# A norm's first unit multiplied by x times scale: token factor and bias applied behind PSUM

## The reference

```python
def rmsnorm(x, w):
    r = lax.rsqrt(jnp.mean(x32 * x32, axis=-1, keepdims=True) + EPS)
    return (x32 * r).astype(x.dtype) * w

def modulate(h, shift, scale):
    return h * (1 + scale) + shift

def swiglu(h, w_i, w_o):
    g, u = jnp.split(h @ w_i, 2, axis=-1)
    return (jax.nn.silu(g) * u) @ w_o
...
    xl = xl + 0.5 * g1l * swiglu(modulate(rmsnorm(xl, norm_w[0]), sh1l, sc1l), w_ffn1_in, w_ffn1_out)
```

## Time and profile before

| | us |
|---|---|
| median of 3 runs | 2497.06 |
| lowest, highest | 2493.27, 2498.05 |
| profiled execution | 2492.84 |
| its span | 2491.0 |

### The profile page before, as it was taken

How to read it: one execution, slowest core, us unless ns; L and a number is a source line. 1 busy time by engine, 2 the same in 40 slices (tenths; PEclk the granted TensorE clock), 3 DMA queues, 4 the chain that set the end, 5 groups by cost and what they waited for, 6 DMA issues and landing times.

```text
span 2491.0 us, 31535 instructions
## 1 busy us (share of the span) xinstructions
PE 2345.1 (94%) x12784; PEld 1886.1 (76%) x12784; DVE 1146.9 (46%) x1970; ACT 829.7 (33%) x1305; POOL 171.3 (7%) x114
## 2 busy tenths in 40 slices
PE   5999999999999999999999999999997996889998
PEld 3777777775777777777777787689996885658888
DVE  2233222437643222233332224775544767457984
ACT  3222222324342222223222224354444454332233
POOL 1000001014000000000000010310011003000001
PEclk7999999999999999999999998999998997789999
DMA  6444444220124444434444422324552221013433
GB/s 262 172 177 178 176 176 191 84 98 17 52 106 178 181 176 170 177 146 152 179 178 176 159 104 100 119 85 170 187 194 90 90 103 49 1 39 144 154 139 136
DMA packets 48310, 340.13 MB, mean 137 GB/s; under 512 B 5168, under 2 KB 7216, under 8 KB 7344
## 3 DMA queue, kind: packets, MB, share of 16 engines
q1 hardware_dynamic: 47136, 337.15, 36.2%
q10 hardware_dynamic: 1040, 1.05, 0.1%
HBM read 337.13 MB, written 1.05 MB: 136 GB/s over the span
## 4 chain that ended last, share of the span: by engine, by line
PE 88%; DVE 6%; ACT 2%; issue 1%; DMA 1%; POOL 1%; SPq 0%; ACTq 0%; DVEq 0%; POOLq 0%
PE bank L451 44%; PE bank L459 22%; PE bank L852 6%; PE bank L425 4%; PE bank L480 3%; PE bank L693 1%; DMA raw<-stream 1%; PE bank L672 1%; PE bank L503 1%; PE bank L652 1%; DVE h L1619 1%; PE bank L681 1%; PE bank L649 1%; ACT w_hi L900 1%; PE bank L509 1%
## 5 line engine op out<-in xcount | busy, mean ns | idle before, releaser
L1273 DVE TENSOR_TENSOR w_lo<-raw,w_hi 128x1024 fp32r<-128x1024 f32 (+1 forms) x389 | 469.1, 1206 | 1082.6 <-ACT w_hi L900 1082.0
L900 ACT ACTIVATE w_hi<-raw 128x1024 fp32r<-128x1024 f32 (+1 forms) x389 | 403.4, 1037 | 1176.2 <-PE bank L451 1155.8
L451 PE MATMUL bank<-h_hi,w_hi 128*128 128x512 f32 (+1 forms) x2024 | 704.2, 360 | 2.7 <-DVE h_lo L1495 1.4
L451 PE MATMUL bank<-h_lo,w_hi 128*128 128x512 f32 (+1 forms) x2024 | 695.3, 356 | 0.0
L451 PEld LDWEIGHTS bank<-h_hi,w_hi 128*128 128x128 f32 x2024 | 383.6, 190 | 82.8 <-issue 28.0
L459 PE MATMUL bank<-h_hi,w_lo 128*128 128x512 f32 (+1 forms) x2024 | 430.3, 355 | 5.1 <-DVE w_lo L1273 5.1
L451 PEld LDWEIGHTS bank<-h_lo,w_hi 128*128 128x128 f32 x2024 | 383.9, 190 | 52.7 <-issue 0.5
L459 PEld LDWEIGHTS bank<-h_hi,w_lo 128*128 128x128 f32 x2024 | 341.7, 190 | 58.9 <-DVE w_lo L1273 6.0
L451 PE MATMUL bank<-hidden_hi,w_hi 128*128 128x512 f32 (+1 forms) x880 | 296.4, 351 | 2.5 <-ACT w_hi L900 2.5
L451 PE MATMUL bank<-hidden_lo,w_hi 128*128 128x512 f32 (+1 forms) x880 | 293.4, 348 | 0.0
L451 PEld LDWEIGHTS bank<-hidden_hi,w_hi 128*128 128x128 f32 x880 | 167.2, 190 | 33.5 <-issue 13.2
(11 more groups left out here) (217 smaller groups left out, 1945.4 us busy)
## 6 DMA issues: line engine op xcount, KB each, us to landing
raw<-stream SPq DMA_DIRECT2D x317, 1024.0 KB, 4.8
x<-x_in SPq DMA_DIRECT2D x1, 2048.0 KB, 9.9
consts<-consts_in SPq DMA_DIRECT2D x1, 1136.5 KB, 5.5
x<-ctx_in ACTq DMA_DIRECT2D x1, 1024.0 KB, 6.7
out<-x SPq DMA_DIRECT2D x2, 512.0 KB, 3.0
params<-params_in SPq DMA_DIRECT2D x1, 413.5 KB, 3.0
```

The costliest lines, as they stand in the source:

```text
L451: last = nc.tensor.matmul(acc, w_hi[:, buffer, kc, :], v(first_chunk + kc), start=start and kc == n == 0, stop=False)
L900: nc.scalar.activation(w_hi[:, buffer, 0:chunks, :], raw[at % RING][:, 0:chunks, sub * P:(sub + 1) * P], ACT.Copy)\
L1273: nc.vector.tensor_tensor(w_lo[:, buffer, 0:chunks, :], raw[at % RING][:, 0:chunks, sub * P:(sub + 1) * P], w_hi[:, buffer, 0:chunks, :].b ...
```

## The change

For the five norms, the unit behind the norm is no longer multiplied with the normed operand. Since the token factor r is one number per column, (W·(x·r·s + shift)) = r·(W·(x·s)) + W·shift.

- While `x` is still being updated, ACT rounds `x·scale` to a raw high part (`raw_high`, two instructions a chunk where there are 512 columns) and DVE makes its rest (`raw_low`, two also). They go to an area that is free at the time (`RAW_AREA`).
- `delayed_unit` on PE: the first unit, half by half. Behind each chunk's two w_hi matmuls, and before each w_lo matmul, there is one more of 4 columns with the same weights (`shift_parts`: shift split in two parts, for latent and context), which gives the bias. Between the w_hi and the w_lo part of the first half stands the sum of squares (all eight squares are now added on POOL, so one set of one-column matmuls); behind the first half the spread, as 4 matmuls of 128 columns.
- `delayed_norm` on ACT and DVE: the normed operand is still made, for the second unit on. The factor is first copied from PSUM to SBUF (`norm_scale`, which is the tile `rms`). DVE multiplies the even chunks with it, POOL the odd ones (`scale_odd`), in three buffers (`scaled`). In this loop, behind chunk step 4, stand the second unit's second half (ACT converts it at step 3) and what takes the first unit out of PSUM (`then`, `after_bias`): move the bias, multiply with the factor, add the bias; in a SwiGLU `Silu` on ACT stands between.
- `joint_product` now multiplies the second unit, with its second half four chunks behind (`stagger=4`).
- The first conversion for the delayed unit stands on DVE ahead of the update of chunk 6 instead of behind that of chunk 7.

```diff
+        DELAYED = ["norm20", "norm30", "norm11", "norm21", "norm31"]
...
+            return KC - 1 if name in DELAYED else ADDED - 1
...
+        OPERAND_AREA = {"norm10": 1, "norm20": 0, "norm30": 0, "norm11": 1, "norm21": 0, "norm31": 0, "norm_a": 0}
+        RAW_AREA = {"norm20": 1, "norm30": 1, "norm11": 0, "norm21": 1, "norm31": 1}
...
+            def delayed_unit(name, accs, start, marks):
+                n, t0 = NORM_AT[name], START[name]
+                hi, lo = normed(start, RAW_AREA[name])
+                pe.wait_ge(sem("side_done"), At.turned)
+                if At.biases:
+                    pe.wait_ge(sem("bias_moved"), At.biases)
+                pe.wait_ge(sem("shift_ready"), DELAYED.index(name) + 1)
+                for sub in range(2):
+                    pe.wait_ge(half_high, At.half + 1)
+                    buffer, bias = At.half % 2, bank[TURN_BANK][:, 4 * sub:4 * sub + 4]
+                    for kc in range(KC):
+                        if sub == 0 and kc in (0, KC - 2, KC - 1):
+                            pe.wait_ge(sem("raw_ready"), raw_parts(name, max(kc + 1, KC - 2)))
+                        for k, v in enumerate((hi, lo)):
+                            last = nc.tensor.matmul(accs[sub], w_hi[:, buffer, kc, :], v(kc), start=kc == k == 0, stop=False)
+                            if kc == 0 and k == 0:
+                                last.then_inc(half_begun, 1)
+                            if sub == kc == 0 and k == 1:
+                                last.then_inc(unit_begun, 1)
+                        nc.tensor.matmul(bias, w_hi[:, buffer, kc, :], shift_parts[:, kc, :], start=sub == kc == 0, stop=False,
+                                         skip_group_check=True)
+                    if sub == 0:
+                        pe.wait_ge(sem("square_added"), adds_before(name) + adds(name))
+                        for tc in range((T - t0) // P):
+                            last = nc.tensor.matmul(bank[SUM_BANK][:, tc:tc + 1], square_sum[:, t0 + tc * P:t0 + (tc + 1) * P],
+                                                    ones[:, 0:1], start=tc == 0, stop=True, skip_group_check=True)
+                        last.then_inc(sem("norm_summed"), 1)
+                        At.norms = n + 1
+                    pe.wait_ge(half_ready, At.half + 1)
+                    for kc in range(KC):
+                        nc.tensor.matmul(bias, w_lo[:, buffer, kc, :], shift_parts[:, kc, :], start=False, stop=kc == KC - 1,
+                                         skip_group_check=True)
+                        last = nc.tensor.matmul(accs[sub], w_lo[:, buffer, kc, :], hi(kc), start=False, stop=kc == KC - 1)
+                    if sub == 1 or marks[0] is not None:
+                        last.then_inc(marks[sub], 1)
+                    At.half += 1
+                    if sub == 0:
+                        pe.wait_ge(sem("rinv_ready"), DELAYED.index(name) + 1)
+                        for tc in range((T - t0) // P):
+                            last = nc.tensor.matmul(bank[SUM_BANK][:, tc * P:(tc + 1) * P], norm_rinv[:, tc:tc + 1].broadcast_to([P, P]),
+                                                    ident, start=True, stop=True, skip_group_check=True)
+                        last.then_inc(sem("rinv_spread"), 1)
+                At.biases += 1
...
+                    if n == 0:
+                        delayed_unit(f"norm2{i}", [bank[IN_BANK[m]][:, 0:T - t0] for m in range(2)], t0, [sem(f"latent_sum{tag}")] * 2)
+                    if n == 2:
+                        for last in joint_product([bank[IN_BANK[m]][:, :] for m in (2, 3)], [normed(0)] * 2, await_chunk, stagger=4,
+                                                  first_begins=True):
+                            last.then_inc(sem(f"latent_sum{tag}"), 1)
...
+            def raw_high(name, kc):
+                if kc == 0:
+                    act.wait_ge(sem("scales_ready"), DELAYED.index(name) + 1)
+                act.wait_ge(x_updated, KC * (UPDATED[name] - 1) + kc + 1)
+                for which, a, b in halves(name):
+                    nc.scalar.activation(areas[RAW_AREA[name]][0](kc)[:, a:b], x[:, kc, a:b], ACT.Copy, scale=scales[:, kc, which:which + 1])\
+                        .then_inc(sem("raw_high"), 1)
+            def delayed_norm(name, first, second, after_bias):
+                n, t0 = NORM_AT[name], START[name]
+                for kc in range(ADDED, KC):
+                    raw_high(name, kc)
+                    square(name, kc)
+                nc.scalar.activation(small[:, 72:73], const("eps"), ACT.Sqrt)
+                convert(first, 1)
+                act.wait_ge(sem("norm_summed"), n + 1)
+                nc.scalar.activation(norm_rms[:, 0:(T - t0) // P], bank[SUM_BANK][:, 0:(T - t0) // P], ACT.Sqrt, bias=const("eps"),
+                                     scale=1.0 / D).then_inc(sem("rms_ready"), 1)
+                convert(second, 0)
+                act.wait_ge(sem("rinv_spread"), n + 1)
+                nc.scalar.activation(norm_scale[:, t0:], bank[SUM_BANK][:, 0:T - t0], ACT.Copy).then_inc(sem("scale_moved"), 1)
+                for kc in range(KC + 1):
+                    modulate(name, kc)
+                    if kc == 3:
+                        convert(second, 1)
+                    if kc == 4:
+                        after_bias()
...
+            def raw_low(name, kc):
+                for k, (which, a, b) in enumerate(halves(name)):
+                    hi, lo = (part(kc)[:, a:b] for part in areas[RAW_AREA[name]])
+                    dve.wait_ge(sem("raw_high"), raw_parts(name, kc) + k + 1)
+                    nc.vector.scalar_tensor_tensor(lo, x[:, kc, a:b], scales[:, kc, which:which + 1], hi.bitcast(F32), ALU.mult, ALU.subtract)\
+                        .then_inc(sem("raw_ready"), 1)
+            def delayed_norm(name, first, second, then):
+                n, t0, k = NORM_AT[name], START[name], DELAYED.index(name)
+                convert(first, 1)
+                dve.wait_ge(sem("rms_ready"), n + 1)
+                nc.vector.reciprocal(norm_rinv[:, 0:(T - t0) // P], norm_rms[:, 0:(T - t0) // P]).then_inc(sem("rinv_ready"), 1)
+                convert(second, 0)
+                dve.wait_ge(sem("scale_moved"), k + 1)
+                hi, lo = areas[OPERAND_AREA[name]]
+                before = h_before(name)
+                for kc in range(KC + 2):
+                    if kc < KC and kc % 2 == 0:
+                        if kc >= N_SCALED:
+                            dve.wait_ge(sem("h_ready"), before + kc - N_SCALED + 1)
+                        nc.vector.tensor_tensor(scaled[:, kc % N_SCALED, t0:], x[:, kc, t0:], norm_scale[:, t0:], ALU.mult)\
+                            .then_inc(sem("h_scaled0"), 1)
+                    if 1 <= kc <= KC:
+                        dve.wait_ge(sem(f"h_scaled{(kc - 1) % 2}"), h_scaled(name, kc - 1))
+                        s, b = modulation(name, kc - 1, 0)
+                        target = scaled[:, (kc - 1) % N_SCALED, CTX:]
+                        nc.vector.tensor_scalar(target, target, s, b, ALU.mult, ALU.add).then_inc(sem("h_lat_ready"), 1)
+                    if kc >= 2:
+                        c = kc - 2
+                        dve.wait_ge(sem("h_high"), before + c + 1)
+                        nc.vector.tensor_tensor(lo(c)[:, t0:], scaled[:, c % N_SCALED, t0:], hi(c)[:, t0:].bitcast(F32), ALU.subtract)\
+                            .then_inc(sem("h_ready"), 1)
+                    if kc == 4:
+                        convert(second, 1)
+                        then()
...
+                def delayed_products():
+                    dve.wait_ge(sem("pair_ready"), UP * f + 1)
+                    move_bias()
+                    nc.vector.tensor_tensor(squares[:, 0, t0:], bank[PAIR_BANKS[0][0]][:, 0:T - t0], norm_scale[:, t0:], ALU.mult)\
+                        .then_inc(sem("gate_scaled"), 1)
+                    own.link(nc.vector.tensor_tensor(squares[:, 3, t0:], bank[PAIR_BANKS[0][1]][:, 0:T - t0], norm_scale[:, t0:], ALU.mult))
+                    dve.wait_ge(sem("bias_moved"), DELAYED.index(norm_name) + 1)
+                    dve.wait_ge(sem("silu_ready"), UP * f + 1)
+                    for which, a, b in halves(norm_name):
+                        last = nc.vector.scalar_tensor_tensor(squares[:, 0, a:b], squares[:, 3, a:b], delayed_bias[1][which], squares[:, 0, a:b],
+                                                              ALU.add, ALU.mult)
+                        own.mark(last) if which else None
+                    own.wait(own.n)
+                    last.then_inc(sem("pair_moved"), 1)
...
+                    elif delayed:
+                        convert(AT[THEN[norm_after]], 0)
...
+                    older = n - 2
+                    if delayed and older >= 0 and older // 2 % len(GROUPS) == len(GROUPS) - 1:
+                        raw_low(norm_after, 2 * (older // 2 // len(GROUPS)) + older % 2)
```

(23 more changed lines are left out.)

## The result

The ratio is 1.0053, with a 95% interval of 1.0041 to 1.0066: 13.2 us slower by the ratio; the two medians are 13.9 us apart. The forecast was "slower", +10.8 us, at 2507.9. The eight times of the changed kernel lie in two groups, four from 2503.38 to 2504.10 and four from 2510.04 to 2512.49, so the median falls between them, and the profiled execution, 2510.04 us, is one of the upper four.

The account below looks back on a forecast made before the run. PE, busy 94%, was the bound, with time to be had only in its waits; five norm stretches going from 157.3 to 168.1 us gave +10.8, so 2503.6, plus 4.2 for the median: 2507.9 (8 in 10: 2494 to 2517).

Follow-up runs that it names:

- e4: The changed kernel with 28 of the 32 4-column matmuls left out of each of the five first units; ratio to the kernel before the change 1.0035.
- e3: The changed kernel with the first unit's way out behind the whole loop and all chunks multiplied on DVE, none on POOL; ratio to the kernel before 1.0028.
- e7: The changed kernel with filler matmuls (13, or 22 at norm31) in each second unit ahead of the wait for the fourth h_lo; ratio to the kernel before 1.0029.
- e9: The changed kernel with fillers ahead of the fourth h_lo, plus twice 6 filler matmuls in norm21's first unit; ratio to the kernel before 1.0031.
- e10: The changed kernel, all five norms, with way out behind the loop, all chunks on DVE, and fillers in the remaining waits; ratio to the kernel before 0.9983.

## What to carry to other kernels

To delay a norm behind the first unit removes PE's wait only if the engine that makes the operand has nothing else in its loop: list what that engine must do between the norm and the operand's last chunk, and put all that nobody waits for behind it. A gain on PE ahead of a wait for another engine is worth little (e4: 28 matmuls fewer, some 3.4 us a norm by their turns, 0.9 gained). Where PE must wait a known time, count the low clock behind the wait as a part of its price (0.9 to 1.3 us here), and measure with fillers what it is. And time a kernel often, and read its untouched parts, before a few us are believed: one kernel gave 1.0065 in four times and 1.0034 in nine.

## What the runs showed of the hardware

The time of untouched work varies with the clock. Two rows of PE's timeline bound a piece of the second block's mixer, before and after the change:

```profile
2078.02 1.22 PE L745 MATMUL bank<-h 128*128 128x256 f32 x2 [7.95 <-DVE h L1630]
...
2202.47 2.07 PE L823 MATMUL bank<-arena,consts 4*128 4x512 f32 x2 [5.71 <-DVE arena L1719]
```

```profile
2093.42 0.80 PE L864 MATMUL bank<-h 128*128 128x256 f32 x1 [7.95 <-DVE h L1926]
...
2214.64 2.07 PE L942 MATMUL bank<-arena,consts 4*128 4x512 f32 x2 [5.70 <-DVE arena L2015]
```

It takes 124.45 us before and 121.22 after, though nothing of it is changed. Windows of the two kernels, 18 us behind its start:

```profile
2096.00:2126.00 30.00, 16.46 (x85) 15.09 (x84) 29.01 (x36) 7.64 (x4) 11.16 (x5) 0.61 0.00 1
```

```profile
2111.00:2141.00 30.00, 18.18 (x87) 17.41 (x86) 28.49 (x35) 7.64 (x4) 11.56 (x5) 0.73 0.00 0
```

Here PE waits for DVE again and again, before the change 2.95 to 4.27 us each time, and DVE is busy nearly throughout. In one execution the clock was granted at 0.61 in the mean and in the other at 0.73. Over the profiles of this case the same piece took 120.3 to 125.4 us. The piece behind it, to the sum of the next norm, is the same work too: 48.6 us in seven profiles, among them before the change, with the clock at 0.79, and 51.9 to 52.3 in the other seven, among them the change, at 0.72. All that stands behind the last stretch took 795.2 us (e4) to 806.3 (e3, e7). Times of one kernel lie 6 to 9 us apart before the change and 15 in e3 and e9; up to 11 us can come from this untouched part, and single stretches of the trace told more than single times. With fillers and the way out behind the loop (e10) the times lay 7.5 us apart. That the clock makes all of the spread was not tried.

A matmul of 4 columns between wide ones costs 0.12 us, of which 0.03 is its own turn and 0.09 a longer turn of the one behind.
